# Moving eight gate units of a hybrid decoder step from the recurrence's chunk loop into the prompt attention

## What is computed

```
proj = rmsnorm(x) @ w_in                 # split into qa, ka, va, qi, ki, wi, ga, gb and the rwkv columns
o_a  = sparse attention (top-k mask from the indexer), 8 heads of 128;
       prompt: 256 queries on 256 keys; sample: 8 sequences on 1024 cached keys in 8 pages, and their own
o_b  = rwkv7(...)                        # 16 heads of 64, a state [64, 64] per head, then group norm and gate
mixed = sigmoid(ga) * (o_a @ w_pa) + sigmoid(gb) * (o_b @ w_pb)
x = x + mixed @ w_o ; x = x + swiglu(rmsnorm(x)) ; out = rmsnorm(x)
```

## Time and profile before

| | us |
|---|---|
| three runs | 2376.16, 2379.64, 2384.27 |
| median | 2379.64 |
| the profiled execution | 2383.22 |
| its span | 2381.3 |
| TensorE busy | 2142.9 (90% of the span) |
| VectorE busy | 1034.6 (43%) |
| ScalarE busy | 712.1 (30%) |

### The profile page before, as it was taken

The page is one execution under the profiler, slowest core; times in us unless marked ns, Lnnn a source line. Parts: engine busy times, 40 slices in busy tenths (PEclk is TensorE's granted clock), DMA queues, the critical chain, the costliest instruction groups (busy, mean ns, idle before and its releaser), DMA issues.

```text
span 2381.3 us, 39247 instructions
## 1 busy us (share of the span) xinstructions
PE 2142.9 (90%) x15718; PEld 1884.9 (79%) x15718; DVE 1034.6 (43%) x1219; ACT 712.1 (30%) x874; POOL 76.1 (3%) x133
## 2 busy tenths in 40 slices
PE   5999754899989985989899999799999999999996
PEld 5999541487747853545799999799999999999996
DVE  4445951587442245100445434544444444333333
ACT  3434011111002231000444423344444444233332
POOL 0000025110000000000000000000000000000000
PEclk9999856789979976888899999899999999999998
DMA  5443242234334414989244545244444444444452
GB/s 184 159 162 129 97 157 51 73 81 155 139 120 124 135 32 165 376 326 361 102 171 161 184 168 186 106 159 168 167 160 174 159 167 167 165 160 168 161 166 88
DMA packets 92315, 376.93 MB, mean 158 GB/s; under 512 B 30290, under 2 KB 33042, under 8 KB 64722
## 3 DMA queue, kind: packets, MB, share of 16 engines
q1 hardware_dynamic: 61298, 330.90, 39.2%
q0 software_dynamic: 7328, 24.18, 3.3%
q10 hardware_dynamic: 23616, 20.78, 2.8%
HBM read 359.25 MB, written 16.53 MB: 158 GB/s over the span
## 4 chain that ended last, share of the span: by engine, by line
PE 80%; DVE 8%; issue 4%; DMA 3%; ACT 2%; SPq 1%; POOL 1%; POOLq 1%; DVEq 0%; ACTq 0%
PE ps L392 13%; PE ps L869 12%; PE ps L870 12%; PE ps L871 12%; PE ps L828 4%; PE ps L830 4%; PE ps L829 4%; PE ps L419 2%; PE ps L418 2%; PE ps L420 2%; PE ps L769 2%; PE ps L801 1%; PE ps L813 1%; PE ps L538 1%; DVE hT L1291 1%
## 5 line engine op out<-in xcount | busy, mean ns | idle before, releaser
L1717 DVE TENSOR_TENSOR weights_lo<-ring,weights_hi 128x2048 fp32r<-128x2048 f32 (+1 forms) x152 | 305.6, 2011 | 467.3 <-ACT weights_hi L1234 467.3
L869 PE MATMUL ps<-h_hi,weights_hi 128*128 128x288 f32 x1408 | 415.2, 295 | 15.4 <-DVE h_lo L1726 15.4
L870 PE MATMUL ps<-h_lo,weights_hi 128*128 128x288 f32 x1408 | 416.9, 296 | 0.0
L871 PE MATMUL ps<-h_hi,weights_lo 128*128 128x288 f32 x1408 | 413.2, 293 | 0.0
L392 PE MATMUL ps<-hT,ring 128*128 128x288 f32 x1472 | 381.5, 415 | 4.6 <-issue 2.5
L1234 ACT ACTIVATE weights_hi<-ring 128x2048 fp32r<-128x2048 f32 (+1 forms) x152 | 257.0, 1691 | 343.8 <-PE ps L871 342.3
L392 PEld LDWEIGHTS ps<-hT,ring 128*128 128x128 f32 x1472 | 277.6, 193 | 86.3 <-issue 12.0
L869 PEld LDWEIGHTS ps<-h_hi,weights_hi 128*128 128x128 f32 x1408 | 264.9, 188 | 15.8 <-DVEq L1741 15.8
L871 PEld LDWEIGHTS ps<-h_hi,weights_lo 128*128 128x128 f32 x1408 | 265.8, 189 | 0.0
L870 PEld LDWEIGHTS ps<-h_lo,weights_hi 128*128 128x128 f32 x1408 | 265.1, 188 | 0.0
L869 PE MATMUL ps<-act_hi,weights_hi 128*128 128x288 f32 x704 | 209.8, 298 | 4.8 <-DVE act_lo L1751 4.8
(11 more groups left out here) (336 smaller groups left out, 3146.0 us busy)
## 6 DMA issues: line engine op xcount, KB each, us to landing
ring<-in_wst SPq DMA_DIRECT2D x201, 1024.0 KB, 4.7
ring<-in_wdn SPq DMA_DIRECT2D x64, 704.0 KB, 4.0
arena<-in_kT SPq DMA_DIRECT2D x64, 512.0 KB, 5.6
arena<-in_v SPq DMA_DIRECT2D x64, 512.0 KB, 5.9
ring<-in_wst ACTq DMA_DIRECT2D x8, 1024.0 KB, 8.1
arena<-chunk_ar_bk ACTq DMA_DIRECT2D x27, 256.0 KB, 3.6
chunk_ar_bk<-arena POOLq DMA_DIRECT2D x2, 2048.0 KB, 10.5
arena<-in_ki POOLq DMA_DIRECT2D x64, 64.0 KB, 2.0
```

Source lines behind the costliest of these rows:

```text
L869: mm(out, W_HI[:, (u - U_FF) % 2, w], hi, start=start, stop=False)
L870: mm(out, W_HI[:, (u - U_FF) % 2, w], lo, start=False, stop=False)
L871: return mm(out, W_LO[:, u % 4, w], hi, start=False, stop=stop)
L1717: tt(W_LO[:, u % 4, 0:m], raw, W_HI[:, at, 0:m].bitcast(F32), ALU.subtract).then_inc(sem("w_split"), 1)
```

## The change

The first eight gate units leave the chunk loop. A new function `fill` issues tiles of consecutive units, and the prompt attention calls it at the end of each n from 7 on with the next eleven tiles: 11 at n = 7, and so on to n = 17, and the last 7 at n = 18. ScalarE copies a unit's bank at the n in which the unit ends, ahead of its copy for the attention. On SyncE's queue the loads of units `U_GA + 8` to `U_GA + 11` move behind the first sequence's key pages.

```diff
-            units(4, U_GA + 12, unit)
+            units(4, U_GA + 8, unit)
...
             for p in range(NPG):
                 k_page(0, p)
+            units(U_GA + 8, U_GA + 12, unit)
             sp.wait_ge(sem("oa_prompt"), 2 * HA)
...
+            def fill(u0, g0, g1):
+
+                while g0 < g1:
+                    k0 = g0 % KT
+                    k1 = min(KT, k0 + g1 - g0)
+                    tile(u0 + g0 // KT, 0, 0, h_tok, NT, k0, k1)
+                    g0 += k1 - k0
...
             def chunk(i, s):
 
                 n = i * 4 + s
-                tile(U_GA, s, i, h_tok, NT, 0, 4)
...
-                    pe.wait_ge(sem("bank_free"), U_GA + 10)
+                    pe.wait_ge(sem("bank_free"), U_GA + 2)
...
+                if n == 7:
+                    pe.wait_ge(sem("var_out"), CT)
+                if n >= 7:
+                    fill(U_GA, 11 * (n - 7), min(11 * (n - 6), 8 * KT))
...
-                act.wait_ge(sem("unit_read"), n + (U_GA + 1))
-                fn(GA[:, bass.ds(n, 1), :].rearrange("p a n -> p (a n)"), ps[(U_GA + s) % 2][:, 0:NT],
-                   ACT.Copy).then_inc(sem("bank_free"), 1)
...
-            for n in range(2 * HA + 2):
+            for n in range(2 * HA + 3):
...
+                for m in range(8):
+                    if n >= 7 and 11 * (n - 7) < KT * (m + 1) <= 11 * (n - 6):
+                        act.wait_ge(sem("unit_read"), U_GA + m + 1)
+                        fn(GA[:, m, :], ps[(U_GA + m) % 2][:, 0:NT], ACT.Copy).then_inc(sem("bank_free"), 1)
```

More of the change, by code:

```diff
@@ L618, in chunk @@
                 ins.then_inc(sem("turned"), 1)
-                tile(U_GA, s, i, h_tok, NT, 4, 8)
                 pe.wait_ge(sem("sgr_in"), i * 64 + 16 * (s + 1))
@@ L638, in chunk @@
                 ins.then_inc(sem("x_done"), 1)
-                tile(U_GA, s, i, h_tok, NT, 8, 11)
                 pe.wait_ge(sem("sti_in"), i * 128 + 32 * (s + 1))
@@ L649, in chunk @@
                 ins.then_inc(sem("u_done"), 1)
-                tile(U_GA, s, i, h_tok, NT, 11, 13)
                 pe.wait_ge(sem("u_out"), 2 * n + 2)
@@ L667, in chunk @@
                 ins.then_inc(sem("chunk_done"), 1)
-                tile(U_GA, s, i, h_tok, NT, 13, KT)
             with pe.Fori(0, 2) as i:
@@ L1152, in _ @@
                        accum_out=ROWSUM[:, n % 2, :]).then_inc(sem("pexp"), 1)
-                if n >= 2:
+                for m in range(8):
+                    if n >= 7 and 11 * (n - 7) < KT * (m + 1) <= 11 * (n - 6):
+                        act.wait_ge(sem("unit_read"), U_GA + m + 1)
+                        fn(GA[:, m, :], ps[(U_GA + m) % 2][:, 0:NT], ACT.Copy).then_inc(sem("bank_free"), 1)
+                if 2 <= n < 2 * HA + 2:
                     m = n - 2
```

## The result

The changed kernel is slower by 0.8%: 2396.94 us, the median of seven runs (2391.72 to 2409.59), against 2384.13 us, the median of seven runs of the kernel before (2376.16 to 2384.69). The ratio is 1.008, its 95% interval 1.005 to 1.011. My forecast of 2401.6 us lies 4.7 us above the median, within the range and on the right side.

What follows compares the result with a forecast made beforehand. TensorE, 80% of the chain and busy for 90% of the span, was taken as the bound. Terms 2 + 31 + 1 + 0.8 - 10.3 - 2.5 = +22 us on 2379.6 gave 2401.6 us, range 2377 to 2422.

Steps and rivals of the forecast that it cites:

- Part 1: Chunk loop without tiles at the full clock: a chunk takes 12.3 us, 3.8 less; 29 us gained in all.
- Part 2: Clock in the chunk loop: falls in the waits, cold chunk 18.1 us, low for two thirds; loop +2 us, gain included.
- Part 3: Tiles in the attention: TensorE becomes the bound from n = 7 to 18, +31; low clock at start +1; exposed end +0.8.
- Part 4: Key pages before the first sequence: issued early enough that the 10.3 us wait goes, -10.3 us.
- rival 4: Key pages still waited for because the group norm ends late: up to +10, 2412 us; no chance of its own.
- late by a hair: First sequence's last value page: there 14.4 us after the attention's end, needed at about 15; no cost, 1 us for range.
- Part 5: First sequence after the attention: starts at the full clock after dense tiles, -2.5 us.
- A clock that survives the waits: Chunk loop: clock stays at 1.00, loop -29 instead of +2, 2370.6 us; chance 0.15.
- A clock that is low throughout: Chunk loop: clock low through the whole loop, +16 instead of +2, 2416 us; chance 0.22.
- The transposes: Chunk loop: by the page's rule transposes don't count as activity, so the clock would hardly rise; no row told.

Runs made afterwards that it cites:

- The first profile: First profiled execution of the changed kernel, code unchanged, slowest of its seven runs: 2409.59 us, chunk loop 141.4 us against 132.7 before.
- The third execution: Changed kernel run again with the same code, its third profiled execution: 2399.97 us, chunk loop 123.1 us.
- The second set: Changed kernel, same code, on another chip against the kernel before: median of four runs 2408.3 us against 2383.96, ratio 1.009.

## Why the prediction was right, point by point

- **Part 1, the chunk at the full clock** (12.3 us): right in its steps, about 0.7 us too long. The waits that I read from the copies as 1.9, 0.9 and 0.9 us are 1.85, 0.84 and 0.87. No chunk with open waits ran at the full clock from end to end: the one of 12.83 us in the kernel with tiles left out is cold at both ends. With the tiles behind it, a chunk runs warm from 745.36 to 754.01, 8.65 us, and with 2.95 us for the last three groups at the full clock that is an estimate of 11.6 us. I had counted a restart of 0.25 us behind the last group, where there is no wait, and rounded up. The 12.33 us with the waits filled come near my figure only because the tiles are 0.4 us longer than the waits. The load of the gram matrices, at worst 0.7 us by my reckoning, makes no chunk of the changed kernel wait, but 1.15 and 1.27 us where the waits are filled and 2.0 us in one chunk with the tiles left out.
- **Part 2, the cold chunk and the mix** (18.1 us; loop +2): right in mechanism and, on average, in size. The cold chunk takes 18.20 us, but that agreement is partly luck: the small groups grow by 1.92/1.08 = 1.78 and not by 1.65, 0.8 us more, and that makes up for the 0.7 us of part 1. The six profiled executions with this loop (four of the changed kernel, one with the value pages first, one with the tiles left out) have 141.4, 131.0, 123.1, 141.4, 133.8 and 133.9 us, a mean of 134.1, which is +1.4 on 132.7. The first profile alone has +8.7. The 1 us that I added for the first chunk wasn't there: it takes 18.20 us cold and took 19.09 before. That the same code covers most of my range from one execution to the next (123 to 141 us) was not in my text. The share of the low clock is near the two thirds that I took: a mean clock of 0.60 is 0.50 for four fifths of the time, and 0.72 is 0.50 for just over half. Where I was wrong is the picture of the mix: I expected whole chunks of 12 and 18 us. The third execution has five that are near that (18.2, 12.8, 18.2, 12.8, 12.8), but the commonest chunk is one of 17.0 us, which has the full clock for one short stretch. Nor does the clock always fall in a wait: in the warm chunks of 12.83 us it outlives all three and falls in the last groups.
- **Part 3, +31 us from n = 7 on, +1 for a cold start, +0.8**: the first is 29.9 us, at 6.44 us for an n instead of 6.6. The cold start didn't show: at 892.04 the first 22 records take 5.50 us, the full clock's price. The handover is the 0.80 us at L770.
- **Part 4, the key pages** (-10.3): -9.5 with the handover in it, and rival 4 is out, since L770 waits for ScalarE and not for the pages. For the value pages, "late by a hair" was the right reading and the wrong size. I had them 14.4 us after the attention's end and needed at 15. They were needed 14.7 us after it (981.41 - 1.83 - 964.90) and there at 16.5: SyncE started to issue them 1.4 us after the end, and the last one landed 7.2 us after the last issue. The next sequence's key pages, queued behind them at 975.32, came later too. I hadn't followed the queue that far.
- **Part 5, the first sequence** (-2.5): the entry is at the full clock as expected, 4.7 us from 965.67 to 970.36 instead of 7.74. The whole first sequence, to the next L770, takes 28.05 us instead of 26.34: 3.0 us less at the entry and 1.4 less at L821 (1.95 against 3.33 us before), but 1.83 and 4.11 us of waits. The term fails in sign, by 4.2 us. It lacked these waits, of which the queue's order makes up 1.6 us; all eight sequences together are 1.4 us shorter.
- **The rivals.** A clock that survives the waits (2370.6 us) is out: PEclk is 0.60 over the loop, and 0.72 at best. That is the rival to which the Trainium skill's page ("TensorE: Matmul & The Clock Gate", section "HAM oscillation — how this bites in real kernels") leads, with its warning of longer gaps only; the measurement decides: here the clock fell in chunk after chunk whose longest wait is 1.85 us, and with the waits filled it did not. The one longer gap, which I hadn't foreseen, is 3.43 us at the turn. With the waits filled and the clock at 1.00 for most of the loop, the kernel takes 2369.86 us, near that rival's 2370.6. That is luck: the loop is 22.9 us shorter than before and not 29, and the rest 9.4 us longer and not 20. A clock that is low throughout (2416) is out: it would need a loop of 149 us, and the longest of these six takes 141.4.
- **The transposes** (the Trainium skill, same page, Part 4, "PE-mode transpose"), which I had left open: by the page they don't count as work in the same way. In the first profile after the change, the 3.68 us of transposes from 848.12 run at the low clock, and the window behind them is up again.

```profile
848.00:852.00 4.00, 3.88 (x18) 3.71 (x19) 0.06 (x1) 0.00 (x0) 0.57 (x1) 0.50 0.50 189
852.00:856.00 4.00, 1.32 (x8) 0.76 (x5) 0.75 (x1) 2.65 (x6) 0.00 (x0) 0.87 0.00 0
```

  In 848 to 852 us, TensorE does little but transposes, at 0.50, and in the next 4 us, with 1.32 us of work (L685), it has 0.87. That speaks against the rule as far as float32 transposes go. The groups ahead of them (the last chunk's) and L685 behind them may have had their part; no run separates them.
- **The sum.** On the profiled executions +26.3 us came where +22 was forecast: the loop +6.7 more than its term, the attention from n = 7 on 2.1 less (29.9 against 31 + 1), the handover with the key pages as forecast, and the other rows of the table together -2.8 where I had -2.5. On the medians it is +12.8 beside the seven runs of before, or +17.3 on the median of 2379.64 from which I started. So the forecast of the change is 9 us too high, and the 4.7 us between the forecast time and the median are so few only because my starting point lay 4.5 us low. The second set, on another chip, gives +24.3. With the mean loop of six executions (+1.4) in place of +8.7, the stages of the profile would give +19.

What stays open: what decides, in one execution, whether the loop takes 123 or 141 us, and why the sequences take 207.9 to 222.0 us across these kernels.

## What to carry to other kernels

Tiles between small dependent groups do two things: they get done, and they keep the granted clock up; take them out and the waits that they covered cost twice, as time and as clock (here 60 us of work left out of the loop made the kernel no faster). Measure how much independent work a wait holds (here 4, 2 and 2 tiles of 0.5 us for waits of 1.85, 0.84 and 0.87 us) and put about that much there. Work beyond it lengthens the stage: before, 16 tiles in a chunk took 16.08 us where eight took 12.33. And moved work is hidden under another engine's bound only up to that engine's pace.

## What the runs showed of the hardware

- Being busy did not raise the clock. TensorE was busy for 3.51 of 4 us on 64-row matmuls (752 to 756 us) and stayed at 0.50. Over the whole loop 107.91 of 142 us busy went with 0.60; in the kernel with full-size tiles in the waits, 45.92 of 48 us went with 1.00.
- A loop can fall in step with the clock. Chunk after chunk of 17.0 us repeats the same short stretch at 2.4 GHz, and the same program needs 123.1 to 141.4 us for one loop, where the kernel before, with its waits covered, and the two profiles with added tiles in the attention alone have 132.7, 133.1 and 132.9.
- The turn from the loop's first pass to its second leaves TensorE idle for 3.43 us that the profile puts down to no wait ("issue"); before, the chunk ahead of the turn was 2.8 us longer than the others. From the changed kernel's timeline, the first transposes behind the turn:

```profile
778.33 1.94 PE L622 MATMUL ps<-cst,arena 128*128 128x128 f32 x8 [3.43 <-issue]
```
